# Adding up the squares of the norms to one chunk on VectorE in a two-block decoder kernel

## What is computed

```
def rmsnorm(x, g):
    xf = x.astype(F32)
    y = xf * lax.rsqrt(jnp.mean(xf * xf, axis=-1, keepdims=True) + EPS)
    return y.astype(x.dtype) * g
```

## Time and profile before

| | |
|---|---|
| median of 3 runs | 907.74 us (906.03 to 907.77) |
| the profiled execution, device time | 907.05 us |
| its span, first to last instruction | 905.4 us |
| TensorE busy | 896.5 us, 99% |
| VectorE busy | 645.1 us, 71% |
| ScalarE busy | 491.9 us, 54% |
| GpSimd busy | 44.2 us, 5% |

### The profile page before, as it was taken

One profiled execution on the slowest core, in us unless ns is written; L12 is line 12 of the kernel. 1 busy time (PEld: TensorE's weight loads), 2 busy tenths in 40 slices (PEclk: granted clock), 3 DMA queues, 4 the chain that ended last, 5 costly groups with the idle time before them and its releaser, 6 DMA issues.

```text
span 905.4 us, 18707 instructions
## 1 busy us (share of the span) xinstructions
PE 896.5 (99%) x7899; PEld 868.8 (96%) x7899; DVE 645.1 (71%) x1182; ACT 491.9 (54%) x841; POOL 44.2 (5%) x50
## 2 busy tenths in 40 slices
PE   8999999999999999999999999999999999999998
PEld 7999999999999998789999999999988999999998
DVE  6887657877767689775887767677678486565664
ACT  6663555564545566674665545547437455444451
POOL 1000001000000000000100001001132000000000
PEclk9999999999999999999999999999999999999999
DMA  9643344565464543722546554554162255555541
GB/s 353 248 172 115 135 159 139 215 232 195 160 219 181 209 152 121 276 94 94 194 177 258 194 202 177 216 203 146 43 232 94 77 208 215 199 187 198 204 157 47
DMA packets 25570, 160.68 MB, mean 177 GB/s; under 512 B 2960, under 2 KB 4880, under 8 KB 6800
## 3 DMA queue, kind: packets, MB, share of 16 engines
q1 hardware_dynamic: 24912, 158.45, 47.3%
q10 hardware_dynamic: 576, 1.05, 0.3%
HBM read 158.18 MB, written 1.05 MB: 176 GB/s over the span
## 4 chain that ended last, share of the span: by engine, by line
PE 94%; DVE 3%; ACT 1%; DMA 1%; issue 0%; SPq 0%
PE ps L395 92%; PE ps L411 1%; DMA raw<-in_w 1%; DVE wl L1247 1%; ACT arena L2306 0%; ACT wh L2034 0%; DVE arena L1675 0%; SPq L2532 0%; DVE arena L1974 0%; DVE arena L1691 0%; DVE arena L1745 0%; ACT arena L2064 0%; DVE arena L1962 0%; DVE arena L1302 0%; ACT L2306 0%
## 5 line engine op out<-in xcount | busy, mean ns | idle before, releaser
L1247 DVE TENSOR_TENSOR wl<-raw,wh 128x1024 fp32r<-128x1024 f32 x282 | 331.5, 1223 | 127.2 <-ACT wh L2034 127.2
L395 PE MATMUL ps<-xh,wh 128*128 128x256 f32 (+1 forms) x1264 | 352.1, 279 | 2.0 <-DVE wl L1247 1.2
L395 PE MATMUL ps<-xl,wh 128*128 128x256 f32 (+1 forms) x1264 | 350.1, 277 | 0.0
L395 PE MATMUL ps<-xh,wl 128*128 128x256 f32 (+1 forms) x1264 | 350.0, 277 | 0.0
L2034 ACT CAST wh<-raw 128x1024 fp32r<-128x1024 f32 x282 | 279.0, 1048 | 120.4 <-PE ps L395 108.3
L395 PEld LDWEIGHTS ps<-xh,wh 128*128 128x128 f32 x1264 | 237.4, 188 | 4.5 <-issue 2.3
L395 PEld LDWEIGHTS ps<-xl,wh 128*128 128x128 f32 x1264 | 237.4, 188 | 0.0
L395 PEld LDWEIGHTS ps<-xh,wl 128*128 128x128 f32 x1264 | 237.4, 188 | 0.0
L395 PE MATMUL ps<-fh,wh 128*128 128x256 f32 x528 | 145.7, 276 | 0.0
L395 PE MATMUL ps<-fl,wh 128*128 128x256 f32 x528 | 145.7, 276 | 0.0
L395 PE MATMUL ps<-fh,wl 128*128 128x256 f32 x528 | 145.7, 276 | 0.0
(11 more groups left out here) (248 smaller groups left out, 1050.6 us busy)
## 6 DMA issues: line engine op xcount, KB each, us to landing
raw<-in_w SPq DMA_DIRECT2D x145, 1024.0 KB, 4.8
raw<-in_w ACTq DMA_DIRECT2D x4, 256.0 KB, 5.4
xt<-in_x SPq DMA_DIRECT2D x4, 256.0 KB, 6.2
arena<-in_mem SPq DMA_DIRECT2D x1, 1024.0 KB, 9.1
out<-xt SPq DMA_DIRECT2D x8, 128.0 KB, 1.9
arena<-in_sel SPq DMA_DIRECT2D x3, 256.0 KB, 6.1
small<-in_small SPq DMA_DIRECT2D x1, 623.0 KB, 5.6
memkv<-in_gmask SPq DMA_DIRECT2D x1, 512.0 KB, 9.9
```

The lines of the kernel that those rows point to most:

```text
L395: return pe.matmul(out, lhsT, rhs, start=start, stop=stop, skip_group_check=True)
L1247: v.tensor_tensor(L[:, s], src[:, s], f32(H[:, s]), ALU.subtract).then_inc(*w_lo.up(2 * S[i] + a))
```

## The change

VectorE makes one more addition per norm: behind the six it adds `sq2[1]` onto `sq2[0]`, after a wait for its own last addition. TensorE's `sums` waits for that addition alone and makes two matmuls instead of four, each of them starting and ending its own column. The semaphore now counts 7 steps per norm instead of 6.

```
@@ def sums
-            for c in range(2):
-                t.wait_ge(*s_sum.at(6 * r + 4 + c))
-                for n in range(2):
-                    last = mm(P[:, n:n + 1], sq2[c][:, n * 128:(n + 1) * 128], cn("inv", 0, 1), c == 0 and n == 0, c == 1)
+            t.wait_ge(*s_sum.at(7 * r + 6))
+            for n in range(2):
+                last = mm(P[:, n:n + 1], sq2[0][:, n * 128:(n + 1) * 128], cn("inv", 0, 1), True, True)
             last.then_inc(*ps.full(name))
@@ def square_sums
                 if c >= 4:
-                    d.wait_ge(*s_sum.at(6 * r + c - 4))
+                    d.wait_ge(*s_sum.at(7 * r + c - 4))
                 acc = sq2[c % 2]
-                v.tensor_tensor(acc[:, 0:T], acc[:, 0:T], sq2[2 + c % 2][:, 0:T], ALU.add).then_inc(*s_sum.up(6 * r + c - 2))
+                v.tensor_tensor(acc[:, 0:T], acc[:, 0:T], sq2[2 + c % 2][:, 0:T], ALU.add).then_inc(*s_sum.up(7 * r + c - 2))
+            if 7 in chunks:
+                d.wait_ge(*s_sum.at(7 * r + 5))
+                v.tensor_tensor(sq2[0][:, 0:T], sq2[0][:, 0:T], sq2[1][:, 0:T], ALU.add).then_inc(*s_sum.up(7 * r + 6))
@@ def squares
             if c >= 4:
-                a.wait_ge(*s_sum.at(6 * NORM[tag] + c - 4))
+                a.wait_ge(*s_sum.at(7 * NORM[tag] + c - 4))
```

## The result

The changed kernel took 903.6 us (median of 7 runs, 903.27 to 905.58), the kernel before, over 7 runs, 906.14 us (905.71 to 907.77). The ratio is 0.9968, with a 95% interval of 0.9959 to 0.9977: faster by 0.3%, more than the 0.2% that can be told from no change. The median of three that the sum was set upon, 907.74, was 1.6 us above what seven runs give.

What follows compares the result with a forecast made beforehand. The prediction took TensorE's list to bound the kernel nearly everywhere. Removed matmuls 2.70 us, less 0.31 at mem and 0.10 at B, gave a gain of 2.29 us and a forecast of 905.2 us, range 903.6 to 907.4.

Steps and rivals of the forecast that it cites:

- What is removed: Two matmuls, four records of 0.112 us, leave TensorE's list at each of six norms: 0.45 us each, 2.70 us in all.
- What is added: One VectorE addition per norm, 0.44 us, hidden behind ScalarE's cast in five norms with 0.07 us left.
- The wait at mem: At the norm mem, TensorE's sums wait 0.31 us for the seventh addition, leaving 0.14 us of gain there.
- B: At the norm B, VectorE is full behind the sums, so only some 0.35 of 0.45 us passes: minus 0.10.
- The level: Starting time for the whole kernel: profiled execution 907.05 us, shown median 0.69 us above it and not wholly trusted.
- rival (3): Half-clock stretch at 392.0 to 395.4 us: without it 903.9 us, chance 0.09; one more 0.05, further ones 0.04.
- (1): Before 352 us, savings become a longer TensorE wait for VectorE at 364.2 us: 0.90 us left, 906.8, chance 0.12.
- (2): At the norms' groups, removed matmuls cost next to nothing: gain 0.6 us in all, 907.1 us, chance 0.05.
- (4): The wait of mem comes in every norm: gain 0.8 us, 906.9 us, chance 0.03.

Runs made afterwards that it cites:

- x5: The kernel before with eight matmuls per norm instead of four, the extra results read by nobody: 911.92 us, ratio 1.0061.
- x6: The changed kernel with two more additions behind the seventh at every norm but A, nobody waiting for them: 905.26 us, ratio 0.9982 to the kernel before.
- y2: The same edit as x6 on the changed kernel, run once more in a later series: 904.36 us, ratio 0.9982 to the kernel before.
- x3: The changed kernel with the seventh addition and its wait, but still four matmuls per norm: 906.63 us, ratio 1.0005 to the kernel before.
- x4: The changed kernel with the sums of mem put behind the first half of the unit m0v0: 903.1 us, ratio 0.9974 to the kernel before.
- y1: The changed kernel itself, unedited, timed again in the last series: 903.73 us, ratio 0.9974 to the kernel before.
- x1: The changed kernel itself, unedited, timed again in the first series: 903.83 us, ratio 0.9976 to the kernel before.
- x2: The changed kernel with two matmuls per norm but without the seventh addition, the second chunk's squares left out: 903.7 us, ratio 0.9973 to the kernel before.

## Why the prediction was right or wrong

**What is removed: right.** 0.45 us a norm, from steps of 0.112 us. Seen as 0.45, 0.44, 0.43 at A, f0 and B, as 0.45 between landmarks to f1, and doubled by x5 as 0.90 for twice as much. What was weighed against it from the Trainium skill, "VectorE: DVE Perf Modes", section on the TRN2 errata (a one-column matmul at 60 cycles), makes an estimate of 25 ns a record; that is near the 30 ns of the records with 16 stationary columns, and far from the 112 ns of those with 128. The figure in the section LDWEIGHTS of the Trainium skill's "TensorE: Matmul & The Clock Gate", 107 ns for 128 columns, comes near these.

**What is added: right.** 0.43 us measured for 0.44, and the cover of five norms was there, with 0.05 us left for 0.07. That a rest at B and nothing else would mind is shown by x6 and y2.

**The wait at mem: right in place and size.** 0.28 us for 0.31, once. x3 has it alone, x4 removes it.

**B: 0.10 us was lost, but not where I had put it.** VectorE's queries start at 348.24 in the changed kernel, 0.09 us behind the start of the small instruction ahead of them (348.15), not behind its end at 348.31. I had set VectorE's earliest start at that end. The 0.37 us of idle time was therefore 0.07 us longer in truth, and what B saves passed the scores: y1 is ahead of x3, which lacks only the saving, by 2.20 us at landmark B and by 2.20 us where the first scores start (349.42 and 351.62). From there to the sums of f1 (445.72 and 447.81) the lead falls to 2.09. So some 0.1 us is given back later in layer 1, in small steps and at no wait that the traces list; why stays open. That the amount agrees with the term is luck.

**The level: wrong, and this is the step that failed.** The steps were summed on the profiled execution (907.05) and set against a median of three (907.74). I distrusted that median, but by 0.25 us only: the level that the 2.29 us were taken from was 907.49, when the seven runs give 906.14. The profiled execution itself showed why, in the earlier trace rows: it had a stretch of half clock that costs 1.4 to 1.5 us, and the sum had no term for it. In the later series 19 of 62 executions of the kernel before had a fall, so a median over many lies among those without; a sum made on an execution with a fall starts from the wrong level. The same rows gave me rival (3), the fall that comes no more, at 903.9 us with a chance of 0.09. Its price was good (1.3 to 1.7 us, for 1.4 to 1.5 near 392 us in traces, 0.76 for the one at 384 us, and 1.25 to 1.65 between the full spans of the kernel before and those with a fall). Its chance was not: the changed kernel had a fall in 7 of 22 executions (the first seven, x1 and y1), about as often as the kernel before, so whether a median has one in it is no property of the change, and the likeliest state was the one without. At 907.05 - 1.4 - 2.3 = 903.35 the same working would have come within 0.3 us of the measured time.

**The rivals.** (1), the gain given back where VectorE ends last, did not happen: TensorE's longest wait for a rest, the one at 364 us, is still 1.0 us, as in the earlier trace rows, and both engines came forward by 1.17 us. (2) is out by x5. (4), a wait in every norm, is out too: it came at mem alone, and there it was shorter than what the matmuls save. (3) is the one that came, as said above.

## What to carry to other kernels

Where one engine's list is full, price an edit by the step from start to start, and look for what the moved work delays by laying its ready time beside the time that the full engine arrives: five of six places had room, and the sixth ate two thirds of its gain. Before summing on a profiled execution, ask whether it is a typical one: a granted clock just under 1 is a term of its own, larger here (1.4 us) than half of the whole change. And a wait that a change brings at one place can often be had back by letting the waiting work stand one unit later, as in x4.

## What the runs showed of the hardware

A float32 matmul with a stationary operand of 128x128 and one moving column takes two records of 0.112 us each; a projection's record, with the same stationary shape and 256 columns, steps by 0.11 to 0.12 us as well, and a record with 16 stationary columns and one moving column by some 30 ns. The granted clock falls to half, for 3.4 us at a time, in a part of the executions of one and the same kernel: it did in 19 of 62 of the kernel before. In the seven traces that have a fall it begins between 390.9 and 392.2 us in six, at 384.2 us in one, each time not more than 1.4 us after the end of an idle time of TensorE of 0.43 to 0.64 us; y1's trace has the same idle times and no fall. The one at 384 us cost 0.76 us, those near 392 us 1.4 to 1.5. The start of the program varies too: the sums of A, ahead of which none of the edits changes TensorE's list, begin between 21.14 us (x2) and 22.10 us (x5).
